# Both mixers' output projections cut into three float32r terms, all units of one mixer ahead of the other's

## The reference

```python
y_sb = stick_breaking_attention(...).reshape(b, l_pad, C_SB)
y_rw = ((group_norm_heads(y_rw, ...) + bonus).astype(h.dtype)) * g
merged = (jax.nn.sigmoid(gate_sb) * (y_sb @ w_sb_out[layer])
          + jax.nn.sigmoid(gate_rw) * (y_rw @ w_rw_out[layer]))
h = h + merged @ w_out[layer]
```

## Time and profile before

| what | value |
|---|---|
| median of 3 runs | 2409.2 us (2403.49 to 2417.78) |
| the profiled execution, its own time | 2407.05 us |
| its span | 2405.2 us, 42199 instructions |
| mean granted clock of TensorE | 0.994 |
| busy: TensorE, DVE, ACT, POOL | 2351.6, 1694.5, 1284.1, 570.6 us |

### The profile page before, as it was taken

The page is one execution under the profiler, slowest core; times in us unless marked ns, Lnnn a source line. Parts: engine busy times, 40 slices in busy tenths (PEclk is TensorE's granted clock), DMA queues, the critical chain, the costliest instruction groups (busy, mean ns, idle before and its releaser), DMA issues.

```text
span 2405.2 us, 42199 instructions
## 1 busy us (share of the span) xinstructions
PE 2351.6 (98%) x16475; PEld 2098.7 (87%) x16475; DVE 1694.5 (70%) x3088; ACT 1284.1 (53%) x2780; POOL 570.6 (24%) x434
## 2 busy tenths in 40 slices
PE   8998999999999999999999999999999999999997
PEld 7878989997899889999888888789989999888886
DVE  5745354446789778887776556869888888777556
ACT  6543345456555665455555555655665455555554
POOL 3626235555379000000000003368300000000000
PEclk9999999999999999999999999999999999999999
DMA  5311155554245556556776564245556655777664
GB/s 192 115 62 55 45 179 180 185 184 147 79 153 183 185 184 196 196 195 207 240 248 217 192 215 150 80 158 175 182 187 192 197 194 190 244 243 238 193 201 140
DMA packets 148086, 420.99 MB, mean 175 GB/s; under 512 B 15920, under 2 KB 49072, under 8 KB 147504
## 3 DMA queue, kind: packets, MB, share of 16 engines
q1 hardware_dynamic: 144080, 405.34, 52.1%
q0 software_dynamic: 2192, 8.99, 1.0%
q10 hardware_dynamic: 1616, 3.96, 0.4%
HBM read 400.40 MB, written 17.83 MB: 174 GB/s over the span
## 4 chain that ended last, share of the span: by engine, by line
PE 93%; DVE 3%; ACT 2%; DMA 1%; issue 0%; POOL 0%; ACTq 0%; DVEq 0%; SPq 0%
PE pb L462 92%; PE pb L471 1%; ACT arena L1234 1%; DVE arena L1754 0%; DVE arena L1751 0%; ACT arena L1422 0%; DMA cst<-in_consts 0%; DMA raw<-in_vT 0%; ACT hi L1222 0%; DMA raw<-in_w_out 0%; DVE sm L2086 0%; DVE H L1751 0%; ACT HT L1520 0%; DVE arena L1902 0%; DVE arena L2218 0%
## 5 line engine op out<-in xcount | busy, mean ns | idle before, releaser
L462 PE MATMUL pb<-HT,hi 128*128 128x256 f32 (+2 forms) x5232 | 1093.8, 302 | 2.5 <-POOL lo L2502 1.9
L1222 ACT CAST hi<-raw 128x512 fp32r<-128x512 f32 x1402 | 817.4, 619 | 373.7 <-PE pb L462 203.0
L462 PEld LDWEIGHTS pb<-HT,hi 128*128 128x128 f32 x5232 | 840.1, 191 | 41.6 <-issue 2.8
L462 PE MATMUL pb<-HT,lo 128*128 128x256 f32 (+1 forms) x2968 | 839.7, 283 | 0.0
L2502 POOL TENSOR_TENSOR lo<-raw,hi 128x512 fp32r<-128x512 f32 x384 | 525.7, 1392 | 465.2 <-ACT hi L1222 464.9
L1761 DVE TENSOR_TENSOR lo<-raw,hi 128x1024 fp32r<-128x1024 f32 x464 | 567.0, 1222 | 41.4 <-ACT hi L1222 41.2
L462 PEld LDWEIGHTS pb<-HT,lo 128*128 128x128 f32 x2968 | 567.2, 191 | 0.0
L462 PE MATMUL pb<-hi,WH 128*128 128x512 f32 x1112 | 433.3, 390 | 0.9 <-DVE WL L2439 0.9
L462 PE MATMUL pb<-lo,WH 128*128 128x512 f32 x1112 | 432.9, 389 | 0.0
L462 PE MATMUL pb<-hi,WL 128*128 128x512 f32 x1112 | 432.7, 389 | 0.0
L2509 POOL DMA_DIRECT2D arena<-in_ln_g x4 | 2.2, 562 | 1263.1 <-PE pb L462 1263.1
(11 more groups left out here) (200 smaller groups left out, 1999.5 us busy)
## 6 DMA issues: line engine op xcount, KB each, us to landing
raw<-in_uT SPq DMA_DIRECT2D x256, 512.0 KB, 3.6
raw<-in_vT SPq DMA_DIRECT2D x256, 512.0 KB, 3.8
raw<-in_w_ffn_in SPq DMA_DIRECT2D x44, 512.0 KB, 3.8
raw<-in_wq SPq DMA_DIRECT2D x32, 512.0 KB, 3.5
wk<-kept SPq DMA_DIRECT2D x128, 128.0 KB, 3.8
raw<-in_w_in SPq DMA_DIRECT2D x24, 512.0 KB, 3.8
raw<-in_w_ffn_out SPq DMA_DIRECT2D x22, 512.0 KB, 4.3
raw<-in_w_gate SPq DMA_DIRECT2D x16, 512.0 KB, 3.2
```

The source lines that it names most:

```text
L462: return e.matmul(o, l, r, start=start, stop=stop)
L1222: e.copy(u.hi[k], u.half[k]).then_inc(*s.up("hi", ("hi", g)))
```

## The change

`SIDES` now has the four units of sbo first and then the four of rwo. All eight are cut like other units, sbo with both lower halves on POOL, rwo with one on DVE and one on POOL. The banks are 4, 5 for g = 0, then 6, 7, then 0, 1 and 2, 3 (`SIDE_BANK`). The activations are cut into `YS`: chunks 0 and 1 of YSB into `WH` and `WL` right after YSB is there, chunks 2 and 3 into chunks 0 and 1 of `HT` after gate 15, and y into chunks 4 to 7 of `HT`. On TensorE the first two sbo units are done for chunks 0 and 1 first, then for chunks 2 and 3; the other six one after the other. `mix` starts when the fifth unit has been taken, and the casts of mixes 0 and 2 wait until the last reader of the storage in `HT` is done. SP waits for the subtraction of the unit three back in all cases. On DVE `take` of gates 14 and 15 is moved behind y.

```diff
--- before.py
+++ after.py
@@ -25,7 +25,8 @@
 NEG = -1e30
 BLK = [(0, 16), (16, 128), (144, 128)]
 
-SIDES = [("sbo", 0), ("sbo", 1), ("rwo", 0), ("rwo", 1), ("sbo", 2), ("rwo", 2), ("sbo", 3), ("rwo", 3)]
+SIDES = [("sbo", g) for g in range(4)] + [("rwo", g) for g in range(4)]
+SIDE_BANK = (4, 6, 0, 2)
 HEADS = [0, 4, 1, 5, 2, 6, 3, 7, 8, 12, 9, 13, 10, 14, 11, 15]
 TILES = (9, 5, 6, 7, 8)
 SCORES = ((0, 1), (6, 7), (0, 1), (4, 5), (0, 1), (4, 5), (0, 1), (6, 7))
@@ -160,7 +161,7 @@
     for g in range(16):
         add(("gate", g), d["w_gate"][g], low=pool)
     for name, g in SIDES:
-        add((name, g), d["w_" + name][g], cut=False)
+        add((name, g), d["w_" + name][g], low=pool if name == "sbo" else both)
     for c in range(8):
         add(("out", c), d["w_out"][0, c * 128:(c + 1) * 128, :], low=pool if c < 3 else both)
     for j in range(23):
@@ -293,6 +294,9 @@
 
         self.XN = ar(0, 2048).rearrange("p (t n) -> p t n", t=2)
         self.SG = [ar(2048 + i * 256, 256) for i in range(2)]
+        pairs = [[T[n][:, i * 256:(i + 1) * 256] for n in ("WH", "WL")] for i in range(2)]
+        self.YS = [pairs + [[h[:, c, :] for h in self.HT] for c in range(2)],
+                   [[h[:, 4 + c, :] for h in self.HT] for c in range(4)]]
         self.AC = [[T[n][:, i * 256:(i + 1) * 256] for n in ("WH", "WL")] for i in range(2)]
         self.TY = [ar(30000 + i * 256, 256) for i in range(2)]
         self.ST6 = sm[:, 72:96].rearrange("p (t k s) -> p t k s", t=2, k=2)
@@ -886,20 +890,26 @@
     gate()
 
 
-    for name, g in SIDES:
-        side = ("sbo", "rwo").index(name)
-        u = units.take(name, g)
-        uv = u.raw.rearrange("p (k c n) -> p k c n", k=2, c=4)
+    def side_part(side, g, u, cs):
+
         for k in range(2):
-            b = 2 * g % 4 + k
-            if side == 0:
+            b = SIDE_BANK[g] + k
+            if side == 0 and cs[0] == 0:
                 emptied(b)
-            w.wait_ge(*s.to("raw", u.i))
-            for c in range(4):
-                w.wait_ge(*(s.to("y", c) if side else s.to("ysb", 7)))
-                x = mm(PB[b][:, side * 256:side * 256 + 256], uv[:, k, c, :], (m.YSB, m.ycv)[side][:, c, :], c == 0, c == 3)
-            x.then_inc(*s.up("part", ("side_ps", g, side, k)))
-            free[b] = [("mixed", g, side, k)]
+            w.wait_ge(*s.to("lo", u.g[k]))
+            for c in cs:
+                w.wait_ge(*s.to("side_lo", side, c))
+                x = mm3(PB[b][:, side * 256:side * 256 + 256], u.chunk(4 * k + c), m.YS[side][c], c == 0, c == 3)
+            if cs[-1] == 3:
+                x.then_inc(*s.up("part", ("part", u.g[k]), ("side_ps", g, side, k)))
+                free[b] = [("mixed", g, side, k)]
+
+    first = [units.take("sbo", g) for g in range(2)]
+    for cs in ((0, 1), (2, 3)):
+        for g in range(2):
+            side_part(0, g, first[g], cs)
+    for name, g in SIDES[2:]:
+        side_part(("sbo", "rwo").index(name), g, units.take(name, g), range(4))
 
     def rows_product(take, lhsT, nk, ready, banks, name, late=None):
 
@@ -1394,6 +1404,9 @@
         w.wait_ge(*s.to("ysb_ps", 7))
         src = PB[b][:, :].rearrange("p (f t) -> p f t", f=2)
         e.copy(m.YSB[:, 2 * (b - 6):2 * (b - 6) + 2, :], src).then_inc(*s.up("sticks", ("ysb", b)))
+    w.wait_ge(*s.to("ysb", 6))
+    for c in range(2):
+        e.copy(m.YS[0][c][0], m.YSB[:, c, :]).then_inc(*s.up("side_hi", ("side_hi", 0, c)))
 
 
     def small_level(lv):
@@ -1478,13 +1491,22 @@
     def mix(g):
         for k in range(2):
             w.wait_ge(*s.to("sum", g, k))
+            if g == 0:
+                w.wait_ge(*s.to("side_ps", 3, 0, 1))
+            elif g == 2:
+                w.wait_ge(*s.to("side_ps", 3, 1, 1))
             e.copy(m.HT[0][:, 2 * g + k, :], m.mt[k][:, 0:256]).then_inc(*s.up("mix_hi", ("mh", g, k)))
 
+    e.copy(m.YS[0][2][0], m.YSB[:, 2, :]).then_inc(*s.up("side_hi", ("side_hi", 0, 2)))
+    e.copy(m.YS[0][3][0], m.YSB[:, 3, :]).then_inc(*s.up("side_hi", ("side_hi", 0, 3)))
     for i, unit in enumerate(SIDES):
         take(*unit)
-        if i in (3, 5):
-            mix(i // 2 - 1)
-    mix(2)
+        if i == 0:
+            for f in range(4):
+                w.wait_ge(*s.to("y", f))
+                e.copy(m.YS[1][f][0], m.ycv[:, f, :]).then_inc(*s.up("side_hi", ("side_hi", 1, f)))
+        if i >= 5:
+            mix(i - 5)
     take("out", 0)
     mix(3)
     for c in range(1, 8):
@@ -1932,6 +1954,9 @@
 
     masks_first(0)
     masks_second(0)
+    for c in range(2):
+        w.wait_ge(*s.to("side_hi", 0, c))
+        tt(m.YS[0][c][1], m.YSB[:, c, :], m.YS[0][c][0].bitcast(F32), S).then_inc(*up("side_lo", ("side_lo", 0, c)))
     masks_first(1)
     small_level(1)
     masks_second(1)
@@ -1969,7 +1994,7 @@
     tt(m.ST, m.ST, m.SC[:, :, 1:2].to_broadcast([128, 4, 64]), M).then_inc(*up("blocks", ("st", 1)))
 
 
-    for g in range(16):
+    for g in range(14):
         take("gate", g)
     for b in (4, 5):
         cs = slice(512 * (b - 4), 512 * (b - 4) + 512)
@@ -1986,13 +2011,22 @@
     own()
     tt(m.ycv, m.ycv, m.BV[:, :, 16:NT], A).then_inc(*up("centre"))
     w.wait_ge(*s.to("gt", 3))
-    own()
+    for c in (2, 3):
+        w.wait_ge(*s.to("side_hi", 0, c))
+        tt(m.YS[0][c][1], m.YSB[:, c, :], m.YS[0][c][0].bitcast(F32), S).then_inc(*up("side_lo", ("side_lo", 0, c)))
+    w.wait_ge(*s.now("centre"))
     for f in range(4):
         tt(m.ycv[:, f, :], m.ycv[:, f, :], m.GT[:, f, :], M).then_inc(*up("centre", ("y", f)))
 
 
+    def side_low(side, src, chunks):
+        for c in chunks:
+            w.wait_ge(*s.to("side_hi", side, c))
+            x = tt(m.YS[side][c][1], src[:, c, :], m.YS[side][c][0].bitcast(F32), S)
+            x.then_inc(*up("side_lo", ("side_lo", side, c)))
+
     def mix(g):
-        bs = (2 * g % 4, 2 * g % 4 + 1)
+        bs = (SIDE_BANK[g], SIDE_BANK[g] + 1)
         w.wait_ge(*s.to("ga", 15))
         w.wait_ge(*s.to("side_ps", g, 1, 1))
         own()
@@ -2008,11 +2042,14 @@
             w.wait_ge(*s.to("mh", g, k))
             tt(m.HT[1][:, c, :], m.mt[k][:, 0:256], m.HT[0][:, c, :].bitcast(F32), S).then_inc(*up("mix", ("mx", c)))
 
+    for g in (14, 15):
+        take("gate", g)
     for i, unit in enumerate(SIDES):
         take(*unit)
-        if i in (3, 5):
-            mix(i // 2 - 1)
-    mix(2)
+        if i == 0:
+            side_low(1, m.ycv, range(4))
+        if i >= 5:
+            mix(i - 5)
     mix(3)
     for c in range(8):
         take("out", c)
@@ -2609,12 +2646,8 @@
     for i, u in enumerate(m.units):
         if i >= RAW:
             before = m.units[i - RAW]
-            if before.cut:
-                w.wait_ge(*s.to("lo", before.g[0]))
-                w.wait_ge(*s.to("lo", before.g[1]))
-            else:
-                name, g = before.name
-                w.wait_ge(*s.to("side_ps", g, 1 if name == "rwo" else 0, 1))
+            w.wait_ge(*s.to("lo", before.g[0]))
+            w.wait_ge(*s.to("lo", before.g[1]))
         elif i:
             w.wait_ge(*s.to("x", 1))
         e.dma_start(u.slot, u.src).then_inc(*s.up(u.slot_key, ("raw", i), by=16))
```

## The result

| | kernel before | changed kernel |
|---|---|---|
| median of 20 runs each | 2408.84 us | 2412.65 us |
| lowest to highest | 2403.02 to 2417.78 | 2406.87 to 2422.92 |
| profiled execution: own time, span | 2407.05, 2405.2 us | 2412.84, 2411.0 us |
| TensorE, DVE, ACT, POOL busy | 2351.6, 1694.5, 1284.1, 570.6 us | 2350.0, 1707.8, 1299.3, 585.6 us |

The ratio is 1.0021, its 95% interval 1.0013 to 1.0029, so the change costs 3 to 7 us. That is under the 0.5% set as a visible difference. The forecast was no visible difference and 2414 us, from a sum of +5.0; the two medians of 20 runs are 3.8 us apart.

What follows compares the result with a forecast made beforehand. TensorE, named for 93% of the span, was taken as the bound; 0.5 + 3.0 + 1.5 + 0 = +5.0 us on 2407.05 gives 2412, plus 2.15 for the median: 2414 us, range 2404 to 2421.

Steps and rivals of the forecast that it cites:

- The rival in which the tensor_scalar do not share: Start of sides: tensor_scalar not sharing, or POOL late to the first turn, gives +1.9 us, 2411; chance 0.18.
- full cover: Start of sides: DVE and POOL pass each other; sides end at 321.9, 2408 us, or 2405 without waits; chance 0.20.
- more waits: Sides or w_out: sbo 3 behind y, or unit 2 of w_out, is late; +8 us, 2417; chance 0.08.
- slower for certain: Sides: units arrive so slowly that TensorE's clock stays at 1.2 GHz throughout; about 2433 us; chance 0.04.
- terms that are no single passes: Side products: each term recorded twice like float32, 192 x 0.43 us = 83 us, giving 2465; chance 0.01.
- What it takes off TensorE: Side products: 192 matmuls at 0.117 us, 22.4 us against 27.5, so -5.1 us if nothing waits.
- Early place: At 162 us: two YSB casts on ACT delay the copy TensorE waits for, +0.5 us.
- Start of the sides: Chunk 2 late at 307.1, TensorE waiting 4.8 us; sides end at 326.8 against 323.8, +3.0 us.
- taken in turn: Start of sides: DVE's tensor_scalar and POOL's subtractions each wait for the other's instruction to end; chunk 2 at 307.1.
- The clock: Between 298 and 307: sparse TensorE work lowers the granted clock, +1.5 us; nothing or twice that as other ends.
- Product with w_out: Behind the sides: at most 0.33 us idle goes, or ACT and DVE about 1 us late; taken as 0.

Runs made afterwards that it cites:

- e1: Changed kernel with POOL subtracting one column instead of 512 in each half of the sbo units, leaving work out; ratio to the kernel before 0.9991.
- e5: Changed kernel with POOL subtracting each half of the sbo units in four pieces of 128 columns; ratio to the kernel before 1.0016.
- e4: Changed kernel with sbo multiplied uncut from raw float32, ahead of rwo in three terms; ratio to the kernel before 1.0026.
- e8: e4 with units ordered sbo 0, 1, 2, rwo 0, 1, sbo 3, rwo 2, 3 and earlier mixing; 2406.62 us, ratio to before 1.0005.
- e2: Changed kernel with 10 and 30 unread matmuls keeping TensorE busy in its waits; 2408.67 us, ratio to the kernel before 1.0014.
- e7: The changed kernel run again, unedited; 2409.75 us, ratio to the kernel before 1.0018.
- e3: Changed kernel with chunks 2 and 3 cast and subtracted earlier, and TensorE doing sbo 0 whole before unit 1; 2408.8 us, ratio to before 1.0011.
- e6: e3 with ACT casting sbo 3 and rwo 0 ahead of y, DVE mixing ahead of its low parts; 2408.35 us, ratio to before 1.0014.
- runs 8 and 9: Run 8: e4 with units reordered and earlier mixing, 2406.62 us; run 9: e4 again, unedited, 2409.29 us.

## Why the prediction was right, and where its terms were not

The time, the forecast of no visible difference and the mechanism came out: a TensorE wait ended by the DVE subtraction into HT at 306.8 (forecast 307.1), tensor_scalar over more than 5 us between POOL's halves, a clock under 1 around 305, sides of 31.6 or 30.6 us (30.5 without the clock, 32.0 with it). That tensor_scalar and POOL hold each other up, and do so by the instruction, e1 and e5 show: the four go 5.33, 1.76, 1.81 us as POOL works whole, not at all, and in pieces. The rule that the prediction cited from the Trainium skill (SBUF — State Buffer, "Who interferes with whom") is an exclusive lock for a whole instruction. The trace agrees with the turns, and not with "whole" if that is the recorded duration: a turn of the two without a pause is 1.27 to 1.29 us where 1.28 and 0.42 make 1.70, and in e5 0.46 us where 0.45 and 0.42 make 0.87. The rival in which the tensor_scalar do not share falls, and so do full cover, more waits, slower for certain, and terms that are no single passes. But several terms were off and partly cancelled, so that the sum of +5.0 comes near the +3.8 to +4.9 of the traces is in part luck.

- **What it takes off TensorE**, -5.1: measured pace 0.120 us and not 0.117 (e1), 23.0 for 27.4 us: -4.4. The products with the side tiles are a little slower than the gates' that the pace came from; why was not tried.
- **Early place**, +0.5: +0.3 (0.95 instead of 0.67 us; 0.67 again in e4 and e8). The casts of 0.72 us overlap the copy ahead of them by 0.1 us, and so does the next copy.
- **Start of the sides**, chunk 2 at 307.1: that is 10.7 us after the sides began, with 2.8 us of work in it, so 7.9 us without work, of which the prediction wrote out 4.8. Measured are 8.8 us (298.01 to 306.84), so 5.9 without work: 4.8 of waits, only 2.9 of them for chunk 2, and the rest half clock and the edges of waits. The step that failed is "taken in turn": it gave each tensor_scalar a POOL subtraction and then its own 0.44 us, 1.7 a turn, where the chain shows 1.24 to 1.51, since the 0.44 lie beside POOL's next subtraction. The four end 5.4 us after the product instead of 6.7. The 10.7 us were 1.9 too large: 1.4 in DVE's chain, and 0.5 since the sides began 0.5 us later (below). At full clock the whole term, forecast +3.0, is about +1.6: 8.8 us to chunk 2 and 168 matmuls at 0.120 make 29.0 for 27.4, and e2 had 29.1.
- **The clock**, +1.5: the stretch at half clock did 33 matmuls in 7.37 busy us, where 33 x 0.120 are 4.0: TensorE's own work is 3.4 us longer in the first profile. Not all of that is on the path, for what runs slowly ahead of the wait for chunk 2 only shortens the wait. From the first product of chunk 2 to the end of the sides the first profile takes 22.8 us (306.84 to 329.65), e7 21.7 (303.22 to 324.95), where 168 x 0.120 are 20.2: +2.6 and +1.6, as the distance to e2 says too (2.5 and 1.5). So the term is right for one execution and 1.1 us short in the other; as one number it was not to be had.
- **Not in the sum**: the square L2005 beside POOL's cut of sbo 0, +0.5 at the start of the sides (44.91 to 45.40 us from the mark; 44.92 in e1 and e5). The prediction placed that cut "in ACT's idle time" and followed ACT only; POOL's half of it was not held against DVE's work at 291. It costs nothing at chunk 2, whose wait is shorter by as much: with it, the sides begin 0.5 us later and are 0.5 us shorter.
- **Product with w_out**, 0: -0.7 in both executions. Of that 0.2 is idle time that went (0.33 to 0.17); for the rest no row names a cause. The late sides may help here: e2, e3, e5 and e6, with sides of 27.1 to 29.6 us, take 23.3 to 23.6 in w_out. e1, without POOL's work on sbo, takes 22.4 even so, and the 25.8 of e4 belong to sbo uncut (runs 8 and 9).
- **Behind w_out**, not in the sum: +0.6, the wait of 1.22 or 1.19 us instead of 0.60 for the next norm, which hangs on the load of a feed-forward unit. The prediction looked no further than w_out.

For the first profile the sum is 0.3 + 0.5 + 4.2 - 0.7 + 0.6 = +4.9 us (4.2 for the sides, 31.6 for 27.4), for e7 +3.8; the medians differ by 3.8, and the ratio stands for 3 to 7.

Where did the gain of the three terms go? 4.4 us come off TensorE's work; 4.8 to 5.4 go into waits, and the clock costs 1.6 to 2.6. Of the waits e1 shows 2.3 to 2.9 us to hang on POOL's work on sbo, and 2.5 to stay without it; e2 shows the clock's part; e5 shows how DVE and POOL hold each other up, but not a shorter stage. Behind the first wait stand others (e3, e6): ScalarE's order, and then DVE's own time. Leaving the first mixer uncut, whose activations are wanted at once and whose weights ACT and POOL must cut around the head norm, is the one form tried that keeps 1.8 us in the two stages, in an order that leaves the mixing steps early, and 0.8 of it at the next norm. That the changed kernel's own order, all sbo first, costs it anything is not shown: no run has the sides cut and in the old order.

## What to carry to other kernels

A term that saves TensorE time by cutting operands moves work to three other engines at one place; before making it, list what each of them is doing in those microseconds, and put the subtraction that TensorE waits for ahead of long chains that it doesn't wait for. Where DVE and POOL overlap, look up in the trace what one meeting costs: here a DVE instruction that met a POOL subtraction of 512 columns took up to 1.1 us longer (tensor_scalar 1.24 to 1.51 for 0.44, the square 2.13 for 1.23, the addition of e6 2.20 for 1.23). Smaller POOL instructions freed DVE but cost POOL. Judge an order of units by the stages behind it as well, up to the next wait that both versions share: what is first finished may be what the next stage needs last, and the next wait may hang on a load that did not move.
